# Values as 64-column tiles of both heads, one key block per visit, and the channel mean and variance inside the output tiles

## What is computed

```python
h = rmsnorm(x, mix_norm[l]); u = h @ w_in[l]
# convolution half, 512 channels
h = a * sigmoid(gate)                    # a, gate: 512 columns of u each
h = depthwise_conv31(h) + conv_b
h = layernorm(h, ln_g, ln_b)             # mean and variance over the 512 channels
y_conv = silu(h)
# attention half: 8 query heads of 64, 2 key/value heads, blocks of 128 tokens
scores = q @ k.T / 8 - slope * |distance|    # own block and its neighbours
p = exp(scores - m); denom = sum(p) + exp(sink - m)
y_attn = (p / denom) @ v
x = x + concat(rmsnorm(y_conv), rmsnorm(y_attn)) @ w_out[l]
```

## Time and profile before

| | us |
|---|---|
| three runs | 1832.73, 1833.85, 1832.9; median 1832.9 |
| the profiled execution | 1833.22, its span 1831.4 |
| PE busy in the span | 1804.5 (99%) |
| POOL, DVE, ACT busy | 1060.7, 884.4, 752.4 |
| matmuls that weigh the values (L1432), 80 records | 37.2 |
| matmuls that spread denominators (L1442), 64 records | 9.1 |

### The profile page before, as it was taken

How to read it: one execution, slowest core, us unless ns; L and a number is a source line. 1 busy time by engine, 2 the same in 40 slices (tenths; PEclk the granted TensorE clock), 3 DMA queues, 4 the chain that set the end, 5 groups by cost and what they waited for, 6 DMA issues and landing times.

```text
span 1831.4 us, 23776 instructions
## 1 busy us (share of the span) xinstructions
PE 1804.5 (99%) x8144; PEld 1485.1 (81%) x8144; DVE 884.4 (48%) x1150; ACT 752.4 (41%) x995; POOL 1060.7 (58%) x535
## 2 busy tenths in 40 slices
PE   9999999999899999999999999999998999999998
PEld 7888888888588888888888888888876888888887
DVE  7544432269776444432254444322797654444212
ACT  6333332246865333332243333222576643333222
POOL 5444457769656444457744444677784854444674
PEclk9999999999999999999999999999999999999999
DMA  5323223322113323223332232334211232322332
GB/s 174 114 92 99 92 78 95 110 98 64 47 47 106 101 92 103 82 79 98 121 103 93 94 101 79 88 96 125 68 52 47 81 103 92 102 93 76 94 95 70
DMA packets 53422, 166.70 MB, mean 91 GB/s; under 512 B 6000, under 2 KB 6256, under 8 KB 53360
## 3 DMA queue, kind: packets, MB, share of 16 engines
q1 hardware_dynamic: 52128, 163.78, 28.6%
q10 hardware_dynamic: 1232, 2.10, 0.4%
HBM read 163.76 MB, written 2.10 MB: 91 GB/s over the span
## 4 chain that ended last, share of the span: by engine, by line
issue 42%; POOL 32%; PE 23%; POOLq 2%; ACT 1%; DVE 1%; DMA 0%; ACTq 0%; DVEq 0%
POOL w_lo L423 26%; PE bank L1249 7%; PE bank L1250 7%; PE bank L1251 7%; POOL y_conv L474 3%; POOL sq_sum L432 2%; POOLq L422 1%; PE bank L1432 1%; POOL x L543 1%; POOL r_wide L499 0%; DVE glu L1182 0%; POOLq L436 0%; PE bank L1442 0%; PE bank L1285 0%; POOLq L443 0%
## 5 line engine op out<-in xcount | busy, mean ns | idle before, releaser
L423 POOL TENSOR_TENSOR w_lo<-stage,w_hi 128x1024 fp32r<-128x1024 f32 x352 | 866.8, 2463 | 705.9 <-ACT w_hi L562 705.8
L562 ACT ACTIVATE w_hi<-stage 128x1024 fp32r<-128x1024 f32 x352 | 372.6, 1060 | 892.4 <-PE bank L1251 891.0
L1249 PE MATMUL bank<-xs_hi,w_hi 128*128 128x512 f32 (+1 forms) x1696 | 660.5, 389 | 0.0
L1251 PE MATMUL bank<-xs_hi,w_lo 128*128 128x512 f32 (+1 forms) x1696 | 656.7, 387 | 0.0
L1250 PE MATMUL bank<-xs_lo,w_hi 128*128 128x512 f32 (+1 forms) x1696 | 656.6, 387 | 0.0
L1250 PEld LDWEIGHTS bank<-xs_lo,w_hi 128*128 128x128 f32 x1696 | 318.6, 188 | 66.3 <-issue 1.9
L1249 PEld LDWEIGHTS bank<-xs_hi,w_hi 128*128 128x128 f32 x1696 | 318.6, 188 | 66.1 <-issue 1.9
L1251 PEld LDWEIGHTS bank<-xs_hi,w_lo 128*128 128x128 f32 x1696 | 318.5, 188 | 65.0
L873 DVE TENSOR_TENSOR work<-bank,rstd 128x512 f32<-128x512 f32 x176 | 120.8, 690 | 406.1 <-PE bank L1251 405.6
L1251 PE MATMUL bank<-h_hi,w_lo 128*128 128x512 f32 x704 | 273.9, 389 | 0.0
L1250 PE MATMUL bank<-h_lo,w_hi 128*128 128x512 f32 x704 | 273.9, 389 | 0.0
(11 more groups left out here) (160 smaller groups left out, 1239.6 us busy)
## 6 DMA issues: line engine op xcount, KB each, us to landing
stage<-w_gu SPq DMA_DIRECT2D x176, 512.0 KB, 3.3
stage<-w_down SPq DMA_DIRECT2D x64, 384.0 KB, 3.2
stage<-w_down SPq DMA_DIRECT2D x64, 320.0 KB, 2.9
stage<-w_in SPq DMA_DIRECT2D x24, 512.0 KB, 3.3
stage<-w_out SPq DMA_DIRECT2D x16, 512.0 KB, 3.3
x<-xT ACTq DMA_DIRECT2D x4, 512.0 KB, 6.9
stage<-w_in SPq DMA_DIRECT2D x8, 256.0 KB, 2.7
out<-result SPq DMA_DIRECT2D x8, 256.0 KB, 2.3
```

What stands on the lines that cost most here:

```text
L423: nc.gpsimd.tensor_tensor(w_lo[:, r, :], stage[:, r, :], w_hi[:, r, :].bitcast(F32), ALU.subtract).then_inc(split, 1)
L562: nc.scalar.activation(w_hi[:, r, :], stage[:, r, :], ACT.Copy).then_inc(hi_made, 1)
L1249: nc.tensor.matmul(to, wh, mh, start=first, stop=False)
L1251: return nc.tensor.matmul(to, wl, mh, start=False, stop=last)
```

## The change

- `weigh_values(b, i)` handles one key block i of token block b for both heads: two matmuls of 64 stationary columns that write partitions 0 to 63 and 64 to 127 of `side_bank` (`tile_position`). Visits are set by `WEIGH_AT`, at units 10, 11, 18, 19, 20, 26, 27, 28; the two of the last block come behind the loop. `v` loses its zeros, `pt` has four slots.
- `widen` is gone: `spread_denominators` reads `r_den` as a broadcast of 64 columns, eight matmuls where there were four, at units 13, 21, 25, 31 (before 10, 18, 25, 31). `normalise` is at 16, 22, 28 and behind the loop.
- `LATE_PRODUCTS` has one product every third unit, not every second; ACT's and POOL's weight splits in the loop start one group later.
- `channel_mean` stands between the halves of the first two attention tiles, where the variance stood; the variance is at tile 4, chunk 2, its spread at tile 5, chunk 1; the convolution statistic is at channel tile 2, chunk 1, its spread at channel tile 3, chunk 0.
- On DVE and ACT the steps of the channels move to match, and two small activations into `table_out` load a table ahead of its use.

```diff
-STATS = ["ffn1", "mix", "mean", "var", "attn", "conv", "ffn2"]
+STATS = ["ffn1", "mix", "mean", "attn", "var", "conv", "ffn2"]
+PT_SLOTS = 4
-RECIP_AT = [4, 13, 21, 25]
-WIDEN_IN = [1, 3, 5, 6]
-SPREAD_AT = [10, 18, 25, 31]
-KEEP_AT = [11, 19, 26, 31]
-EVICT_AT = [13, 21, 28, 32]
+RECIP_AT = [4, 13, 19, 23]
+SPREAD_AT = [13, 21, 25, 31]
+KEEP_AT = [14, 22, 26, 31]
+EVICT_AT = [16, 22, 28, 32]
+WEIGH_AT = {10: (0, 0), 11: (0, 1), 18: (1, 0), 19: (1, 1), 20: (1, 2), 26: (2, 0), 27: (2, 1), 28: (2, 2)}
-LATE_PRODUCTS = range(0, 16, 2)
+LATE_PRODUCTS = range(0, 24, 3)
-        LN_BANK = [6, 3, 6, 2]
+        LN_BANK = [6, 3, 7, 2]
...
-                def weigh_values(g):
-
-                    b, kv = divmod(g, 2)
+                def weigh_values(b, i):
+
                     first, n = keys_of(b)
-                    pe.wait_ge(pt_made, l * N_UNITS + (g + 1) * GROUP)
-                    if b and not kv:
+                    pe.wait_ge(pt_made, l * N_UNITS + (b + 1) * 2 * GROUP)
+                    if b:
                         pe.wait_ge(o_evicted, l * NB + b)
-                    for i in range(n):
-                        last = nc.tensor.matmul(side_bank[:], v[:, first + i, kv, :],
-                                                pt[:, g % 2, i, :, :].rearrange("p c q -> p (c q)"),
-                                                start=not kv and i == 0, stop=bool(kv) and i == n - 1)
-                    last.then_inc(o_made, 1)
+                    for kv in range(N_KV_HEADS):
+                        rows = slice(HEAD_DIM * kv, HEAD_DIM * (kv + 1))
+                        last = nc.tensor.matmul(side_bank[rows, :], v[:, first + i, rows],
+                                                pt[:, (2 * b + kv) % PT_SLOTS, i, :, :].rearrange("p c q -> p (c q)"),
+                                                start=i == 0, stop=i == n - 1, tile_position=(0, HEAD_DIM * kv))
+                    if i == n - 1:
+                        last.then_inc(o_made, 1)
 
                 def spread_denominators(b):
 
-                    pe.wait_ge(r_widened, (l * NB + b + 1) * N_KV_HEADS)
+                    pe.wait_ge(r_den_made, l * NB + b + 1)
                     bank_taken(ATT["spread", b, 0])
                     for c in range(GROUP):
-                        last = nc.tensor.matmul(att_bank("spread", b, 0)[:, c * P:(c + 1) * P],
-                                                r_wide[:, c, :, :].rearrange("p h d -> p (h d)"),
-                                                ident[:], start=True, stop=True)
+                        for kv in range(N_KV_HEADS):
+                            rows = slice(HEAD_DIM * kv, HEAD_DIM * (kv + 1))
+                            last = nc.tensor.matmul(att_bank("spread", b, 0)[rows, c * P:(c + 1) * P],
+                                                    r_den[:, 2 * b + kv, c:c + 1].to_broadcast([P, HEAD_DIM]),
+                                                    ident[:], start=True, stop=True, tile_position=(0, HEAD_DIM * kv))
                     last.then_inc(factors_spread, 1)
...
                         if half == 0:
-                            channel_variance()
-                    spread_factors(l, "var")
+                            channel_mean()
...
-                attention_tiles({(2, 1): attention_statistic, (3, 0): lambda: spread_factors(l, "attn")})
-                channel_tiles({(0, 1): conv_statistic, (1, 2): lambda: spread_factors(l, "conv")})
+                attention_tiles({(2, 1): attention_statistic, (3, 0): lambda: spread_factors(l, "attn"),
+                                 (4, 2): channel_variance, (5, 1): lambda: spread_factors(l, "var")})
+                channel_tiles({(2, 1): conv_statistic, (3, 0): lambda: spread_factors(l, "conv")})
...
+                normalise(NB - 1)
+                dve.wait_ge(stat_made, stat_no(l, "mean") + 1)
+                centre(0)
+                for c in range(NC):
+                    split_attention(c, 1)
+                add_result_squares(0)
+                for c in range(1, NC):
+                    centre(c)
+                token_recip(l, "attn")
+                take_rstd(2 * l, spread_no(l, "attn") + 1, "attn")
                 out_a(0)
-                split_channels(0)
+                for c in range(1, NC):
+                    add_channel_squares(c)
                 out_a(1)
                 out_a(2)
...
                 root(l, "attn", by_token=True)
+                for c in range(NC):
+                    square_channels(c)
                 mix_high(16)
+                root(l, "var", by_token=True)
+                nc.scalar.activation(table_out[:], eps[:], ACT.Silu)
+                mix_high(17)
                 for c in range(NC):
                     activate_channels(c)
+                for c in range(NC):
                     square_results(c)
-                mix_high(17)
                 mix_high(18)
```

More of the change, by code:

```diff
@@ L159, in encoder @@
         eps = sb("eps", [P, 1])
+        table_out = sb("table_out", [P, 1])
         gain0 = sb("gain0", [P, ND])
@@ L491, in denominators @@
                                             ALU.add).then_inc(den_made, 1)
-                def widen(b):
-                    pool.wait_ge(r_den_made, l * NB + b + 1)
-                    if b:
-                        pool.wait_ge(factors_spread, l * NB + b)
-                    for kv in range(N_KV_HEADS):
-                        nc.gpsimd.tensor_tensor(r_wide[:, :, kv, :],
-                                                r_den[:, 2 * b + kv, :].unsqueeze(2).to_broadcast([P, GROUP, HEAD_DIM]),
-                                                zero[:, 0:1].unsqueeze(2).to_broadcast([P, GROUP, HEAD_DIM]),
-                                                ALU.add).then_inc(r_widened, 1)
                 def add_channel(c):
@@ L524, in _ @@
                         sink_args(g // 2 + 1)
-                    late = 2 if done < NC * P_TAPS else 0
+                    if g in DEN_IN:
+                        denominators(DEN_IN.index(g))
+                    late = sum(u // GROUP == g for u in LATE_PRODUCTS)
                     add_products(done, late)
@@ L531, in _ @@
                         add_channel(2)
-                    if g in DEN_IN:
-                        denominators(DEN_IN.index(g))
-                    if 3 <= g < 7:
-                        mix_low(12 + g - 3)
-                    if g in WIDEN_IN:
-                        widen(WIDEN_IN.index(g))
+                    if g >= 4:
+                        mix_low(12 + g - 4)
                 for s in range(4):
@@ L721, in _ @@
                 act.wait_ge(v_turned, l + 1)
-                for kv in range(N_KV_HEADS):
-                    at = slice(HEAD_DIM * kv, HEAD_DIM * (kv + 1))
-                    nc.scalar.activation(v[:, :, kv, at], side_bank[:].rearrange("p (b d) -> p b d", d=P)[:, :, at],
-                                         ACT.Copy).then_inc(v_made, 1)
+                nc.scalar.activation(v[:], side_bank[:].rearrange("p (b d) -> p b d", d=P), ACT.Copy).then_inc(v_made, 1)
                 for c in range(3):
@@ L817, in _ @@
             root(DEPTH, "ffn1", by_token=True)
-            act.wait_ge(spread, spread_no(DEPTH, "var") + 2)
+            act.wait_ge(spread, spread_no(DEPTH, "attn") + 2)
             act.wait_ge(root_ready, 1)
@@ L1182, in add_result_squares @@
                         nc.vector.tensor_tensor(of[0], of[0], of[c], ALU.add).then_inc(result_added, 1)
-                token_recip(l, "var")
-                add_result_squares(0)
-                dve.wait_ge(spread, spread_no(l, "var") + 1)
-                for c in range(NC):
-                    scale_channels(c)
-                token_recip(l, "attn")
-                take_rstd(2 * l, spread_no(l, "attn") + 1, "attn")
                 def split_channels(c):
@@ L1199, in split_channels @@
                                                    ALU.subtract).then_inc(y_split, 1)
+                normalise(NB - 1)
[8 more added lines that the diff above has]
+                take_rstd(2 * l, spread_no(l, "attn") + 1, "attn")
                 out_a(0)
-                split_channels(0)
+                for c in range(1, NC):
+                    add_channel_squares(c)
                 out_a(1)
                 out_a(2)
-                for c in range(1, NC):
-                    split_channels(c)
-                    out_a(2 + c)
-                add_result_squares(1)
+                token_recip(l, "var")
+                dve.wait_ge(spread, spread_no(l, "var") + 1)
+                scale_channels(0)
+                scale_channels(1)
+                out_a(3)
+                scale_channels(2)
+                scale_channels(3)
+                split_channels(0)
+                out_a(4)
+                split_channels(1)
+                out_a(5)
+                split_channels(2)
+                split_channels(3)
                 out_a(6)
                 out_a(7)
```

(1 more changed line is left out.)

71 lines of the change are left out of this document (27 added, 44 removed).

## The result

| | before | after |
|---|---|---|
| median, us | 1833.78 (6 runs, 1832.73 to 1833.93) | 1840.77 (6 runs, 1839.58 to 1843.45) |
| ratio | | 1.0043, 95% interval 1.0032 to 1.0053 |
| profiled execution / its span, us | 1833.22 / 1831.4 | 1842.17 / 1840.3 |

The change costs 7.0 us, 0.4%. The forecast was 1842.0, slower. Its sign and size hold, but by luck: two large errors in it cancel. The attention loop gained more than forecast, and TensorE's clock fell to half in places, which was not foreseen.

What follows compares the result with a forecast made beforehand. The prediction took PE, busy 99%, as the bound, except early in the attention loop, where DVE sets the pace. Terms -5.6 + 0.9 + 1.6 + 2.05 + 2.3 + 0.2 + 2.85 = +4.3 us a layer gave 1842.0 us, range 1832 to 1850.

Steps and rivals of the forecast that it cites:

- loop, tiles start earlier: Attention loop: the first output tile starts at 500.4 us in place of 506.1, 5.6 us earlier a layer; ends 2 and 12.
- mean behind the loop: Between the halves of the first output tiles: the mean's float32 matmul adds two records, 0.86 us, which left the loop.
- second half of tile 0: Output tiles after the mean: PE waits for DVE's splits, queued behind centring, +1.6 us a layer.
- variance: At tile 4, chunk 2: DVE's three sums of channel squares stretch beside POOL, +2.05 us; 0 if POOL were idle.
- first channel tile: Channel tiles' start: the first square stands behind four SiLUs and split 0 waits for it, +2.3 us a layer.
- sums of result squares: Statistic at channel tile 2: the sums meet POOL, end 0.4 us after PE wants them, 0.2 more than before.
- channel tile 4: PE arrives at 12.65 us, but the new x's split is done at 15.5 because of the late spread: +2.85 us.
- I take 1.29 us, three slots: Weighing in the loop: a key block's four records on two column halves take three slots, between 0.86 and 1.72 us.
- 0.2 us a change: Weighing visits in the loop: each entry to or exit from 64-column tiles costs 0.2 us, with ends 0 and 0.33.
- rival 1: Loop: heads fully overlap or tile changes cost near nothing; loop gives 8 to 9 us a layer, 1836 us; chance 0.17.
- the forecast's own sign of being wrong: Prediction wrong if the tiles start more than 8 us earlier, or the four output-stage waits are below 4 us a layer.
- Rival 3: Output stage: DVE, ACT and POOL chains end before PE asks; -3 us a layer, 1827 us; chance 0.09.

Runs made afterwards that it cites:

- The one-tile kernel: The changed kernel with both heads' weighing matmuls aimed at the same 64 columns and output rows; 1850.87 us (one run).
- the kernel with two waits filled: The changed kernel with matmuls on zeros, 6 ahead of the wait for the channel squares' sum, 8 ahead of channel tile 4's; 1835.44 us.
- the last experiments: Changed kernel, zeros at channel tile 4, POOL's output-stage work after the channel squares' sums: 1831.43 us; also last sinks' arguments ahead of group 4's weight split: 1827.26 us.
- the kernel with the early channel statistic: The changed kernel with only the variance's wait filled, squares between the SiLUs and the channel statistic one tile earlier; 1836.17 us.
- the statistics half alone: The kernel before with only the mean, channel squares, variance and channel statistic moved, old weighing kept; 1859.49 us, ratio 1.0141.

## Why the forecast was right, and where it was not

Measured times count from start to start, as the forecast's do.

| step, us a layer | forecast | measured |
|---|---|---|
| loop, tiles start earlier | -5.6 | -9.0 |
| mean behind the loop | +0.9 | +0.9 |
| second half of tile 0 | +1.6 | +1.5 |
| variance | +2.05 | +1.9 |
| first channel tile | +2.3 | +2.4 |
| sums of result squares | +0.2 | -0.2 |
| channel tile 4 | +2.85 | +2.6 |
| clock | none | +4.3 (5 stretches of 1.7 in two layers) |
| sum | +4.3 | +4.4 |

The difference between the profiled executions is 1842.17 - 1833.22 = 8.95 us, 4.5 a layer. The steps behind the loop sum to +9.1 without the clock, and the loop gives 9.0: at full clock gain and loss cancel.

**The loop.** Here the step "I take 1.29 us, three slots" failed, and with it "0.2 us a change". A block takes two slots and 0.15 us for both changes. The forecast's list at these prices: six blocks and the last pair give seven slots fewer (3.0 us), seven visits give 0.25 each (1.75), three spreads 0.17 each (0.5). That is 5.3 us earlier than 500.4; the unforeseen wait at the third spread takes 2.0 back, which gives the trace's 497.1. Two more errors cancel in that: the block at unit 18 starts at 478.8 us and not at 480.1, and from there to the tiles the turned blocks take 4.9 us, a wait of 0.4 among them, where the list has 3.8. This was the mechanism of rival 1 ("full overlap, cheap changes"), and the forecast's own sign of being wrong, tiles that start more than 8 us earlier, is there; the other one, waits below 4 us a layer, is not (7.1 us of idle time). Its argument against overlap was the order of starts, taken as if a pass had to wait for the ones listed ahead of it. The one-tile kernel settles it: the same list in the same order, and 0.85 us saved in each block by the second tile. The Trainium skill (TensorE: Matmul & The Clock Gate, Part 3: Packing small matmuls — row/col tiling) gives 2.38x for three column tiles. With this kernel's two tiles and float32 the trace agrees that column tiles run at once: 1.86 against 1.01 us, 1.84x with the changes of tile in it. The Trainium skill (TensorEngine Tiling (Array Packing), Key Properties) states a drain at a change of tiling mode. Here it is no more than 0.15 us for a visit.

**The waits.** The four places, the order of causes behind each and the times hold: DVE's first sum was forecast 15.05 us behind the tiles' start and came at 15.07. Each of the four is within 0.3 us of its term; only the sums of result squares, forecast late by 0.4 us, come 0.2 late, less than before. The contention with POOL, the late squares and the late spread are shown by the runs that take each away or put one in alone. That the mean's centring holds the second half of tile 0 is read from the lists and the trace; no run takes it away.

**The clock.** No term was given for it, since the rows of before had none to show. It is +8.5 us in the profiled execution, as much as the whole forecast. Without it the change would be a draw: the kernel with two waits filled takes 1833.7 to 1834.3 us at full clock, before takes 1833.0. So the direction was right by luck, because of something that the forecast did not contain. By its own terms with the loop at -9.0 the sum would have been 2 x (9.9 - 9.0) = +1.8 us, 1835 us: rival 1, too little to tell from no change.

**Rival 3**, the faster one, said that the chains would be done in time. They were not, as forecast; but the last experiments show how little was missing: with POOL out of the way, 0.2 us of work ahead of a split and zeros in one wait, the kernel is 5.8 us faster than before.

## What to carry to other kernels

When PE is 99% busy, price a new wait twice: its length, and the half-clock stretch that can follow it (here mostly 1.7 us, behind waits of 1.7 to 2.7 us). Where such a wait can't be removed, matmuls on zeros in a free bank that end before the wait does are cheap. When a change has two halves, time each alone; here one half was worth 11 us and the other took all of it back. And when long instructions move in a queue, look for the shortest instruction behind their new place and who waits for it.

## What the runs showed of the hardware

- Two float32 matmuls on different 64-column tiles overlap fully: 1.01 us for four records against 1.86 on one tile. Entering and leaving the tiles costs 0.15 us together.
- PE's clock fell to half behind waits of 1.7 to 2.7 us inside dense work, without a longer idle time ahead, for some 3.4 us and twice for 6.8 (the kernel with the early channel statistic in layer 0, the statistics half alone in layer 1). 3.4 us of it cost 1.7, and the same wait is followed by it in some executions and not in others.
- Three float32 sums of two SBUF tiles on DVE take 4.37 us while POOL works and 2.28 us while it doesn't. The Trainium skill (GPSIMD Engine Reference, 1. Specifications) says that DVE instructions with two SBUF inputs contend with it; the runs agree and give the size.
